# A two-layer diffusion backbone in one kernel: the first projection units multiplied block by block, with the first modulation vectors and the filter pieces among them

## The reference

```
sh1, sc1, g1, sh2, sc2, g2 = split(silu(c) @ w_mod[l] + b_mod[l], 6)     # modulation vectors
xn   = rmsnorm(h, norm1_g) * (1 + sc1) + sh1                             # the same for the context, with c_ctx
proj = xn @ w_in                   # pooling, Hyena, query, key/value and gate columns
filt = [h_fwd, 0, reversed h_bwd] / l1(h_fwd, h_bwd)                     # h = sine MLP(t) * exp(-t |decay|)
b    = x0 * (irfft(rfft(z) * rfft(filt)) + z * hy_bias)
h    = h + g1 * (gated sum of three mixers @ w_out)
h    = h + g2 * (square(relu((rmsnorm(h, norm2_g) * (1 + sc2) + sh2) @ w_ff1)) @ w_ff2)
out  = rmsnorm(h, final_g)
```

## Time and profile before

| what | value |
|---|---|
| median of 3 runs | 1514.2 us (1510.49 to 1516.42) |
| the profiled execution | 1513.88 us, its span 1512.1 us |
| mean granted TensorE clock | 0.978 |
| PE, DVE, ACT, POOL busy | 94%, 53%, 34%, 14% |
| chain that ended last, PE's share | 87% |

### The profile page before, as it was taken

How to read it: one execution, slowest core, us unless ns; L and a number is a source line. 1 busy time by engine, 2 the same in 40 slices (tenths; PEclk the granted TensorE clock), 3 DMA queues, 4 the chain that set the end, 5 groups by cost and what they waited for, 6 DMA issues and landing times.

```text
span 1512.1 us, 19509 instructions
## 1 busy us (share of the span) xinstructions
PE 1416.6 (94%) x8034; PEld 1131.5 (75%) x8034; DVE 794.8 (53%) x1106; ACT 521.1 (34%) x787; POOL 218.3 (14%) x203
## 2 busy tenths in 40 slices
PE   2899999999999999799999999978999899899996
PEld 0365766777877787477777777757868899799996
DVE  3575557433554464643322443346776576776664
ACT  3242245233222131433212332113444453464451
POOL 4300100060301134200000000220003201500012
PEclk9999999999999999899999999997999999999998
DMA  8322220444542125244444445322314463456552
GB/s 329 159 93 74 98 70 1 153 167 167 195 168 70 56 84 181 77 160 153 167 145 148 167 141 180 140 98 84 126 56 150 161 248 125 155 167 195 196 194 71
DMA packets 56584, 210.52 MB, mean 139 GB/s; under 512 B 6213, under 2 KB 7365, under 8 KB 55600
## 3 DMA queue, kind: packets, MB, share of 16 engines
q1 hardware_dynamic: 54176, 194.22, 37.3%
q0 software_dynamic: 2320, 15.05, 2.6%
HBM read 205.58 MB, written 3.67 MB: 138 GB/s over the span
## 4 chain that ended last, share of the span: by engine, by line
PE 87%; DVE 7%; DMA 2%; ACT 2%; POOL 1%; issue 1%; SPq 0%; DVEq 0%; POOLq 0%; ACTq 0%
PE ps L1229 25%; PE ps L1230 24%; PE ps L1231 24%; PE ps L1258 3%; PE ps L1437 2%; PE ps L1462 2%; DVE normed L865 2%; PE ps L1528 1%; PE ps L1538 1%; DMA raw<-in_units 1%; PE ps L1449 1%; DVE wl L813 1%; DVE rstd L858 1%; DVE xl L874 1%; PE ps L1329 1%
## 5 line engine op out<-in xcount | busy, mean ns | idle before, releaser
L1229 PE MATMUL ps<-xh,wh 128*128 128x512 f32 (+2 forms) x1376 | 475.6, 346 | 33.1 <-DVE xl L874 28.8
L813 DVE TENSOR_TENSOR wl<-raw,wh 128x1024 fp32r<-128x1024 f32 x272 | 359.3, 1323 | 251.1 <-ACT wh L590 247.9
L1230 PE MATMUL ps<-xl,wh 128*128 128x512 f32 (+2 forms) x1376 | 467.0, 339 | 0.0
L1231 PE MATMUL ps<-xh,wl 128*128 128x512 f32 (+2 forms) x1376 | 466.1, 339 | 0.0
L590 ACT ACTIVATE wh<-raw 128x1024 fp32r<-128x1024 f32 x272 | 287.0, 1055 | 320.4 <-PE ps L1231 315.7
L1229 PEld LDWEIGHTS ps<-xh,wh 128*128 128x128 f32 (+1 forms) x1376 | 261.3, 190 | 80.0 <-issue 40.3
L1231 PEld LDWEIGHTS ps<-xh,wl 128*128 128x128 f32 (+1 forms) x1376 | 261.9, 190 | 30.6
L1230 PEld LDWEIGHTS ps<-xl,wh 128*128 128x128 f32 (+1 forms) x1376 | 262.2, 191 | 29.1 <-issue 1.0
L1229 PE MATMUL ps<-hid_h,wh 128*128 128x512 f32 (+1 forms) x512 | 172.0, 336 | 0.0
L1230 PE MATMUL ps<-hid_l,wh 128*128 128x512 f32 (+1 forms) x512 | 170.6, 333 | 0.0
L1231 PE MATMUL ps<-hid_h,wl 128*128 128x512 f32 (+1 forms) x512 | 170.3, 333 | 0.0
(11 more groups left out here) (204 smaller groups left out, 1478.1 us busy)
## 6 DMA issues: line engine op xcount, KB each, us to landing
raw<-in_units SPq DMA_DIRECT2D x272, 512.0 KB, 3.3
mod_ring<-in_mod_units SPq DMA_DIRECT2D x80, 512.0 KB, 4.0
first_ring<-in_mod_units SPq DMA_DIRECT2D x16, 512.0 KB, 9.1
filters<-filt POOLq DMA_DIRECT2D x2, 1280.0 KB, 6.2
filt<-filters POOLq DMA_DIRECT2D x2, 1280.0 KB, 10.9
ftab<-in_fwd POOLq DMA_DIRECT2D x3, 768.0 KB, 5.3
h<-in_x POOLq DMA_DIRECT2D x1, 2048.0 KB, 18.2
counts<-in_counts POOLq DMA_DIRECT2D x2, 1024.0 KB, 5.3
```

The source lines that it names most:

```text
L813: dve.tensor_tensor(wl[:, g % SLOTS, :], raw[:, g % SLOTS, :], wh[:, g % SLOTS, :].bitcast(F), ALU.subtract)\
L1229: pe.matmul(dst, w_h, m_h, start=first, stop=False)
L1230: pe.matmul(dst, w_h, m_l, start=False, stop=False)
L1231: return pe.matmul(dst, w_l, m_h, start=False, stop=last)
```

## The change

Four things change.

First, the opening. The first two modulation vectors come in 8 *pairs* instead of 16 units: pair m (1 MB) gives shift and scale of channel block m alone. The tokens are loaded first, by SP in four pieces. ACT squares them, POOL and DVE add them in pairs, and four matmuls sum them. Then the first **four** units (q and the first kv) are multiplied together, block by block: `wave_step(m)` has 12 matmuls. Around each step stand the turn of pair m + 1, the matmuls of pair m + 2 and one tap matmul of the filters.

Second, the filters: each has its own envelope, even and odd buffers; the spectra are copied to the filter unscaled by ACT, and the division by l1 moves to the place where the filter is used. Even, odd and l1 sums go to POOL, and each spectrum is stored by a DMA of its own.

Third, norms 1 to 3: DVE multiplies all 8 blocks by `rstd`, ACT then applies scale and shift (two instructions) and rounds in a third, DVE makes the rest. POOL no longer takes part. The first two units behind each of these norms are multiplied together, block by block.

Fourth, narrow units (kpe, uq, pool_w) are loaded and split in their real width.

```diff
+            for c in range(4):
+                sp.dma_start(h[:, 2 * c:2 * c + 2, :], x_in[:, 2 * c:2 * c + 2, :]).then_inc(h_in_s[c], 16)
...
+            def norm_full(v, m):
...
+                if v == 0:
+                    act.wait_ge(pair_ready, m + 1)
                 for s in range(NORM_T[v] // SEQ):
                     t = slice(s * SEQ, (s + 1) * SEQ)
-                    last = act.activation(xh_of[v // 2][:, m, t], normed[:, m, t], ACT.Identity, bias=mods[:, shift, m, s:s + 1])
-                last.then_inc(x_hi, 1)
+                    last = act.activation(normed[:, m, t], normed[:, m, t], ACT.Identity, bias=mods[:, shift, m, s:s + 1],
+                                          scale=scales[:, v, m, s:s + 1])
+                last.then_inc(x_full, 1)
...
+            for m in range(KB):                      # ACT
+                norm_full(0, m)
+                norm_hi(0, m)
+                if m + 1 < KB:
+                    copy_pair(m + 1)
...
+            for m in range(KB):                      # DVE
+                if m + 1 < KB:
+                    norm_by_rstd(0, m + 1)
+                norm_lo(0, m)
+                if m == 0:
+                    filter_sine_argument(1)
+                elif m >= 2:
+                    filter_weighted(m - 2)
+                if m + 1 < KB:
+                    add_pair(m + 1)
...
+            for m in range(KB):                      # PE
+                if m + 1 < KB:
+                    turn_pair(m + 1)
+                wave_step(0, m, first, T, (x_split, 0))
+                if m + 2 < KB:
+                    pair(m + 2)
...
+                if m >= 2:
+                    filter_taps(m - 2)
...
+            for f in range(DEPTH):                   # POOL
+                filter_parts(f)
+                filter_abs_sum(f)
...
+            def filter_copy(f, i):                   # ACT
+                if f:
+                    act.wait_ge(f_saved[0][i], 16)
+                act.wait_ge(f_spec, 5 * f + i + 1)
+                act.activation(filt0[:, i * HY:(i + 1) * HY], ps[:, 7 - (5 * f + i) % 2, :], ACT.Copy).then_inc(f_copied, 1)
...
+                    if half == "a":
+                        p = PHASES[layer, "ff1a"]
+                        wave(layer, [(p.g0 + j, act_bank(p, j)) for j in range(2)], n, (x_split, KB * (2 * layer + 1)))
```

More of the change, by code:

```diff
@@ L101, in plan @@
     out, g, act, dve, part = {}, 0, 0, 0, 0
-    mod, turn, order = MOD_FIRST, None, [("unit", i) for i in range(MOD_FIRST)]
+    mod, turn, order = MOD_FIRST, None, []
     for layer, name, pattern in _phases():
@@ L679, in _ @@
+            filter_absolutes(1)
+            split(2 * WAVE)
+            for i in range(5):
+                filter_copy(1, i)
             for layer in range(DEPTH):
@@ L845, in straight, with norm_rstd @@
                     mod_events(p, j)
[L847 removed]
+            def norm_rstd(v):
                 n = NORM_T[v]
[L850 to L856 removed]
                 dve.wait_ge(std_ready, v + 1)
@@ new lines, in filter_spectrum @@
+            def filter_spectrum(f, i):
+                part, at = [(f_even[f], 0), (f_even[f], 128), (f_odd[f], 2 * NFREQ), (f_odd[f], NFREQ + 128),
+                            (f_even[f], 2 * NFREQ + 128)][i]
+                o = 5 * f + i
+                if i == 0:
+                    pe.wait_ge(f_parts, 4 * f + 4)
+                if o >= 2:
+                    pe.wait_ge(f_copied, o - 1)
+                for tb in range(2):
+                    mm = pe.matmul(ps[:, 7 - o % 2, :], ftab0[:, tb, at:at + 128], part[:, tb, :], start=tb == 0, stop=tb == 1)
+                mm.then_inc(f_spec, 1)
@@ new lines, in filter_l1 @@
+            def filter_l1(f):
+                pe.wait_ge(f_summed, f + 1)
+                if f:
+                    pe.wait_ge(f_l1_ready, 2 * f)
+                for c in range(HYB):
+                    mm = pe.matmul(ps[:, 5, 64 + HYB * f + c:65 + HYB * f + c], envelope[:, f, 0, c * 128:(c + 1) * 128], ones[:, 0:1],
+                                   start=True, stop=True)
+                mm.then_inc(f_l1, 1)
+            pe.wait_ge(act_bank_free, 2)
+            pe.wait_ge(dve_bank_free, 2)
@@ new lines, in _ @@
+            pe.wait_ge(consts_in_s, 16)
+            for c in range(4):
+                if c < 2:
+                    pe.wait_ge(x_paired_pool, c + 1)
+                else:
+                    pe.wait_ge(x_paired_dve, c - 1)
+                mm = pe.matmul(ps[:, SUMSQ_BANK[0], :], ones, normed[:, 2 * c, :], start=c == 0, stop=c == 3)
+            mm.then_inc(sumsq_ready, 1)
+            pe.wait_ge(f_sin, 1)
+            pe.matmul(ps[:, 7, 0:SEQ], f_w12[:, 1, :], f_hid[:, :], start=True, stop=True).then_inc(f_pre, 1)
@@ new lines, in _, with first_kv, key_pe @@
+            for i in (6, 7):
+                filter_taps(i)
+            def first_kv():
+                p = PHASES[0, "kv"]
+                pe.wait_ge(lo_ready, p.g0 + 2)
+                bank = dve_bank(p, 1)
+                blocks(ps[:, bank, :], (p.g0 + 1) % SLOTS, xh_of[0], xl_of[0], T).then_inc(unit_done, 1)
+            def key_pe(layer):
+                for j, p, slot in straight(layer, "kpe"):
+                    bank = dve_bank(p, j)
+                    for k in range(KB):
+                        mm = three(ps[0:ROPE, bank, :], *cols(slot, k * ROPE, ROPE), xh_of[layer][:, k, :], xl_of[layer][:, k, :], k == 0, k == KB - 1)
+                    mm.then_inc(unit_done, 1)
@@ L1741 @@
         "units": _units(w),
+        "pairs": _pairs(w),
         "mod_units": _mod_units(w),
```

597 lines of the change are left out of this document (349 added, 248 removed).

## The result

The changed kernel took 1521.89 us (median of 5 runs, 1520.81 to 1525.76), the kernel before 1514.2 (5 runs as well): a ratio of 1.0057, with a 95% interval of 1.0036 to 1.0079. It is 0.6% slower; the prediction had 1510.6 us, 0.2% faster. Of all the executions in this document one stands apart, 1829 us at a mean granted clock of 0.745 for the kernel with filled gaps, and it is in no ratio. The profiled execution of after took 1520.81 us with a span of 1519.0, against 1513.88 and 1512.1 before.

A forecast was written before the change was run, and what follows sets the result against it. PE, busy for 94% of the span, was taken as the bound, so only its waits or work removed count. 1513.88 us + 6 (opening) - 9.3 (norms) = 1510.6 us, range 1497 to 1522.

The forecast's parts named there:

- The norms: Norms 1 to 3: earlier first matmuls gain 3.8, 4.4 and 1.1 us, sum 9.3, bounds 0 and 12.
- Rival E: Norms 1 to 3: the three passes on ACT eat the gain, 1519 us; chance 0.10.
- To the first step: Start of the opening: tokens, rstd, block 0 and splits done, so that step 0 starts at 29.6 us.
- Steps 0 to 2: Opening: starts at 29.6, 35.6 and 42.0 us, with the second sine argument and envelope 0 between.
- Steps 2 to 7: Opening: DVE's order makes the chain serial, 10.0 us a step; step 7 starts at 91.2 us.
- the term of 3.9 us from the tap to the next step: Opening steps: drain, weighting, additions, scaled halves, rounding, copy, turn and handoffs, with none of it beside the 12 matmuls.
- The 1.7 us for the clock: Opening: charged to each PE burst behind an idle stretch of 3 us or more, for starting at the low clock.
- From step 7 to the end of the filters: Late opening: step 7 ends at 95.9, taps 99.6, spectra 104.7, filter-copy wait 6.2 us to 130.9, latent sums end at 145.9.
- B: Opening steps: the clock holds through the 3.9 us gaps, six steps save 1.7 us each, 1500 us; chance 0.19.
- C: Opening steps: the clock never rises, steps 1 to 7 each pay 2.4 us more, 1527 us; chance 0.12.
- A: Whole kernel: the forecast as summed, 1510.6 us, own range 1505 to 1516; chance 0.46.
- D: Opening: off-PE chains overlap better than written, 6 us of the 6.2 come back, 1504 us; chance 0.13.

The follow-up runs named there:

- kernel with filled gaps: The changed kernel with ten matmuls more behind the tap of each of steps 2 to 6, which make one unit's sums wrong: 1514.08 us, ratio 1.0012.
- run with the weighting one step later: The changed kernel with VectorE normalising pair m+1 first, then weighting the tap of step m-3 instead of m-2: 1490.76 us, ratio 0.9839.
- the run that keeps it away: The changed kernel with GpSimd's halves of filter 0 held back until all eight pairs are normalised: 1516.0 us, ratio 1.0022.
- two runs with early stores: Filter 0's five stores issued before the sums of filter 1's absolutes: in the changed kernel 1515.33 us, with the weighting one step later as well 1484.73 us.
- kernel with the pair first: The changed kernel with VectorE normalising pair m+1 before weighting the tap of step m-2: 1509.06 us, ratio 0.9977.

## Why the prediction was wrong

**The norms, right in the mechanism, and in the sum by some luck.** 9.3 us forecast, 8.8 in the trace, 8.0 by the medians. Norm 1: 3.8 forecast, 3.7 measured. Norm 2: 4.4 and 3.2. The first kv matmul behind it came 28.4 us after the sums before and 24.2 after, 4.3 us sooner, as forecast, but 1.1 us were lost again ahead of norm 3. Norm 3: 1.1 and 0.2. It started 0.9 us sooner, but 24 of its matmuls ran low, where 18 did before; I had 20 in either case. The three make 7.1 us. The other 1.7 were gained between the gate unit and norm 1 (472.8 us before, 471.1 after), where I had nothing. The kernel before with the new norms gains 1.6 there too (471.2), so it is neither the new opening nor the narrow units; its cause stays open. Rival E (ACT eats the gain) did not come.

**The opening, wrong in size.** Forecast +6, measured +15.7. By the steps of the prediction:

*To the first step*, 29.6 forecast, 31.75 measured, +2.2. The squares ended at 13.15 us, not 9.8, and the reciprocal at 24.96, not 22.4, because the tokens came later: ACT waited for pieces of `in_x` until 10.74, where I had them all landed at 8.7 by the rate of the earlier trace rows. From 3 to 10.7 us the DMAs moved 337 GB/s, not 420, and the tokens shared it with GpSimd's loads, which the forecast left out. VectorE's two additions took 4.04 us beside GpSimd's, which TensorE did not feel, as it ran its sums at the low clock.

```profile
10.74 2.41 ACT L735 ACTIVATE normed<-h 128x512 f32<-128x512 f32 x4 [0.21 <-DMA h<-in_x]
...
12.43 4.04 DVE L1048 TENSOR_TENSOR normed<-normed 128x512 f32<-128x512 f32 x2
...
14.85 6.00 PE L1521 MATMUL ps<-normed,consts 128*128 128x512 f32 x8 [5.28 <-POOL normed L507]
```

*Steps 0 to 2*, 12.4 us forecast, 13.6 measured, +1.2: step 0's wave ran at the low clock.

*Steps 2 to 7*: this is the step that failed. It said "One step is 10.0 us" and had step 7 start 49.2 us behind step 2; it was 54.7, +5.5. The mechanism stood in the text, and the run with the weighting one step later shows that it is the cause. What was mis-sized is the term of 3.9 us from the tap to the next step (its parts add up to 4.0). With the tap it makes 4.8 us; the five were 5.21, 6.32, 4.86, 6.32 and 5.21, 4.3 us more in all. Wave and pair were 1.2 us more. The 1.7 us for the clock held: the five waves lost 7.9 us by it, for 8.5 charged. The size was short in two places. GpSimd beside VectorE is 3.1 us, by the run that keeps it away; I had put 1 us on it for the whole opening. The other 2.4 are in that run too: its steps are 10.3 us, not 10.0, and so is the last one, which I had at 9.0 because no turn stands in it; there TensorE waits for the low parts instead (4.09 us in after, 4.64 in that run).

*From step 7 to the end of the filters*: 8.4 us forecast to the first spectrum, 9.2 measured; 6.8 from there to the second kv unit, 7.5 measured, because a weight split of 2.89 us (my price was 1.2 to 1.3) stood on VectorE in front of the latent, beside GpSimd's products:

```profile
110.45 2.89 DVE L922 TENSOR_TENSOR wl<-raw,wh 128x1024 fp32r<-128x1024 f32 x1
110.94 1.32 POOL L551 TENSOR_TENSOR mod_ring<-envelope 128x512 f32<-128x512 f32 x1
```

Then 24.5 us forecast to the end of the wait for the filter copy (106.4 to 130.9), and 24.5 measured (116.7 to 141.2). The wait itself, 6.2 forecast, was 5.5, and the two runs with early stores show that its cause was the one named. Its size owes something to luck. The parts named for the chain off PE add up to 7.9 us, and the text went on with 9.5 (120.7 to 130.2); measured were 9.2 (131.41 to 140.57), because the sums on POOL took 4.8 us and not 2.6.

The last 15.4 us to the gate unit were forecast as 15.0. The differences, 2.2 + 1.2 + 5.5 + 0.8 + 0.7 + 0.4, are 10.8 us with the rounding, less the 1 us set aside for GpSimd: 9.8, against a gap of 9.7 between 146.9 and 156.6.

**The rivals.** B (1500, the clock holds through the gaps) did not come: the waves of steps 3 to 7, behind waits of 3.16 to 4.33 us, began at the low clock, and only those of steps 1 and 2, behind 0.5 and 1.9 us, ran high throughout. The 10 us that I gave it is near the 9.5 that the low clock cost; the filled kernel, which forces it in part, gained 6.4 us of span. C (the clock never rises, 1527) came half: the granted clock was 0.77 from 31 to 100 us, and several waves ran low to the end. The result of 1521.9 lies between A and C, inside the range (up to 1522) by 0.1 us, which is chance, and over the line of 1521.8 that the text had set for slower by as little. D and E did not come. Where I chose worst was the chance of 0.14 for slower: several terms of the opening (the landing of the tokens, the sums on POOL, the last step) had no row of their own, a collision (clock, GpSimd, queue) could only make them longer, and I had put 1 us on that.

**What I did not ask.** The prediction named the weighting in front of the pair as the chain of the opening, priced the step within 0.3 us of what it is without GpSimd, and stopped there. Its own prices give the step without the chain too: wave 2.7, pair and tap 1.7, turn 0.6, 5.0 us in all, and 5.44 were measured (2.92, 2.05 and 0.47). The change thus holds a gain of 2.0% over the kernel before (1484.7 us), and two orderings that took 31 and 6 us of it away.

## What to carry to other kernels

When work from two chains is interleaved on an in-order engine, the queued instruction must wait only for something that was finished a step ago. Put the consumer one step behind its producer: here that was one index (m - 3 for m - 2), with the pair in front, and worth 31 us. Price an idle gap of TensorE at more than its length (here 19.1 us of gaps brought 9.5 us of low clock with them), and look for GpSimd instructions beside every short VectorE instruction that lies on such a ring. A wave that follows a normalisation block by block needs enough units to cover the time of one block; with one unit the earlier start gained nothing here, by a single execution.

## What the hardware showed

- A VectorE instruction of 128x2 elements took 1.26 us beside a GpSimd product of 1.25 us, against 0.16 alone, and a low part L969 1.76 us against 0.69 (in the kernel with the pair first). In these rows the price goes by what is left of the GpSimd instruction and not by the size of the one that is blocked: the 128x2 operation ended at 64.42 us and the product beside it at 64.39, and in the kernel with the pair first at 62.64 and 62.63.
- Ten 512-column matmuls of no use in each of five gaps shortened the kernel by 6.4 us of span.
- The kernel before varies with the clock too. In the profile of before the eight tap instructions ran low, 7.12 us, though the granted clock is shown as 1.00 from 40 to 60 us there, so the distance of the matmuls is the safer reading; in the profile of the kernel before with the new norms the same ones took 3.70, its gate unit started at 134.26 us and not at 140.91, and this execution (1498.64) was 6.4 us under its median:

```profile
45.08 3.70 PE L1380 MATMUL ps<-f_w,f_hid 64*128 64x512 f32 x8
```

  One profile of an opening is thus good to about 6 us here, and a forecast of half a percent that rests on it has that much doubt before it begins. The medians put the opening's loss at 1521.9 - 1505.0 = 16.9 us (18.7 by the ratios 1.0057 and 0.9933), near the 15.7 of the profiles.
